# Two-block transformer forward on one core: the gated recurrence computed two chunks to a tile, its steps dealt out between tiles of the weight products

## What is computed

```
b = cumsum(log_f) within a chunk                       # chunks; per head, 128 channels
A[t,s] = sum_d q[t,d] k[s,d] exp(b[t,d] - b[s,d]),  s <= t
o = A v + (q exp(b)) S ;  S' = exp(b_last) S + (k exp(b_last - b))^T v
y_hg = rmsnorm(o) * sigmoid(go) * silu(z)
kc, vc = compress(k), compress(v)                      # 31 overlapping blocks, a two-layer MLP
o_cmp = softmax(q kc^T) vc ;  o_nsa = g0 o_cmp + g1 o_selected + g2 o_window
```

## Time and profile before

| | |
|---|---|
| median of 3 runs | 2809.46 us (2808.98 to 2810.98) |
| the profiled execution | 2808.89 us |
| its span, first to last instruction | 2807.1 us |
| mean granted TensorE clock | 0.991 of full speed |
| PE busy | 2705.7 us (96% of the span) |
| DVE, ACT, POOL busy | 1167.6, 1275.7, 1402.6 us |
| PE's part in the chain that ended last | 85% (DVE 6%, issue 4%, ACT 4%) |

### The profile page before, as it was taken

How to read it: one execution, slowest core, us unless ns; L and a number is a source line. 1 busy time by engine, 2 the same in 40 slices (tenths; PEclk the granted TensorE clock), 3 DMA queues, 4 the chain that set the end, 5 groups by cost and what they waited for, 6 DMA issues and landing times.

```text
span 2807.1 us, 41389 instructions
## 1 busy us (share of the span) xinstructions
PE 2705.7 (96%) x13644; PEld 2276.7 (81%) x13644; DVE 1167.6 (42%) x2054; ACT 1275.7 (45%) x2207; POOL 1402.6 (50%) x1801
## 2 busy tenths in 40 slices
PE   8999899999889999999999999999999999999998
PEld 6888778788877888888878888888888887888887
DVE  4768742567874224423242422322442324142232
ACT  5555745655673643444443432324344444343233
POOL 4535554543554453554634655545355463455553
PEclk9999999999999999999999999999999999999999
DMA  5223013322301332233422333333223342233332
GB/s 153 72 50 99 16 39 90 91 61 65 92 1 54 89 110 69 90 98 98 124 87 69 106 104 91 98 98 110 69 90 98 98 124 88 68 106 105 91 98 98
DMA packets 270818, 242.46 MB, mean 86 GB/s; under 512 B 29376, under 2 KB 203648, under 8 KB 270592
## 3 DMA queue, kind: packets, MB, share of 16 engines
q1 hardware_dynamic: 267696, 235.12, 28.9%
q10 hardware_dynamic: 2896, 4.52, 0.5%
HBM read 237.51 MB, written 2.10 MB: 85 GB/s over the span
## 4 chain that ended last, share of the span: by engine, by line
PE 85%; DVE 6%; issue 4%; ACT 4%; DMA 0%; DVEq 0%; POOL 0%; ACTq 0%; POOLq 0%
PE bank L2017 11%; PE bank L2021 11%; PE bank L2020 11%; PE bank L1951 8%; PE bank L1954 8%; PE bank L1955 8%; PE bank L845 4%; PE bank L849 4%; PE bank L848 4%; PE bank L983 2%; PE bank L1906 2%; PE bank L895 1%; PE bank L898 1%; PE bank L899 1%; PE bank L2142 1%
## 5 line engine op out<-in xcount | busy, mean ns | idle before, releaser
L2865 POOL TENSOR_TENSOR wboth<-raw,wboth 128x256 fp32r<-128x256 f32 (+1 forms) x1616 | 1292.3, 832 | 1289.4 <-ACT wboth L2166 1289.1
L2166 ACT CAST wboth<-raw 128x1024 fp32r<-128x1024 f32 (+2 forms) x443 | 455.4, 1034 | 601.2 <-PE bank L2017 401.9
L1951 PE MATMUL bank<-xhi,wboth 128*128 128x512 f32 x928 | 364.2, 392 | 2.1 <-DVE h L2553 1.6
L1955 PE MATMUL bank<-xhi,wboth 128*128 128x512 f32 x928 | 361.4, 389 | 0.0
L1954 PE MATMUL bank<-xlo,wboth 128*128 128x512 f32 x928 | 361.3, 389 | 0.0
L2017 PE MATMUL bank<-wboth,xhi 128*128 128x512 f32 x832 | 326.5, 392 | 3.9 <-DVE xlo L2444 3.9
L2021 PE MATMUL bank<-wboth,xlo 128*128 128x512 f32 x832 | 324.0, 389 | 0.0
L2020 PE MATMUL bank<-wboth,xhi 128*128 128x512 f32 x832 | 323.8, 389 | 0.0
L845 PE MATMUL bank<-wboth,xhi 128*128 128x512 f32 (+2 forms) x672 | 248.2, 369 | 5.5 <-DVE pT L1524 3.1
L848 PE MATMUL bank<-wboth,xhi 128*128 128x512 f32 (+2 forms) x672 | 243.4, 362 | 0.0
L849 PE MATMUL bank<-wboth,xlo 128*128 128x512 f32 (+2 forms) x672 | 243.4, 362 | 0.0
(11 more groups left out here) (512 smaller groups left out, 4878.2 us busy)
## 6 DMA issues: line engine op xcount, KB each, us to landing
raw<-in_w_in SPq DMA_DIRECT2D x147, 512.0 KB, 3.7
raw<-in_w SPq DMA_DIRECT2D x132, 512.0 KB, 3.8
raw<-in_w_pg SPq DMA_DIRECT2D x16, 512.0 KB, 3.8
raw<-in_w_o SPq DMA_DIRECT2D x16, 512.0 KB, 3.8
raw<-in_xa_k SPq DMA_DIRECT2D x16, 512.0 KB, 3.9
raw<-in_xa_v SPq DMA_DIRECT2D x16, 512.0 KB, 3.9
raw<-in_xa_q SPq DMA_DIRECT2D x16, 512.0 KB, 4.1
raw<-in_xa_o SPq DMA_DIRECT2D x16, 512.0 KB, 3.8
```

The costliest lines, as they stand in the source:

```text
L1951: mm = pe.matmul(o, wh, rhs[0][:, k, :], start=(k == 0), stop=False)
L1955: mm = pe.matmul(o, wl, rhs[0][:, k, :], start=False, stop=(k == KD - 1))
L2166: nc.scalar.copy(whi[:, j % SLOTS, 0:nk * cols], raw[:, j % SLOTS, 0:nk * cols]).then_inc(hi_split, 1)
L2865: ins = nc.gpsimd.tensor_tensor(wlo[:, s, part], raw[:, s, part], whi[:, s, part].bitcast(F32), ALU.subtract)
```

## The change

1. **Pairs.** Chunks 0 and 2 are kept in natural order, chunks 1 and 3 reversed in time, in `qT`, `kT` and `bT` (order 0, 2, 1, 3: `PLACE`). At a level the later half of a natural chunk and the later half of a reversed one occupy different halves of a tile, so one 128x128 product serves both chunks. `level_product` makes two products for a level instead of four; `keep` copies 128x256 instead of 128x512 into a sum tile `Ap` (new masks take both corners); `part_chunks` then splits `Ap` into `At` once per head with two COPY_PREDICATED of 128x256. The diagonal keeps four products and takes two copies. The values of the reversed chunks are reversed once by four products with a reversed identity (`v_back`), emptied by four copies on ACT. Copies of q, the exp that makes kT, and the forward decays take two instructions each instead of one.
2. **Dealing.** tm steps of this stretch are split into parts of one token tile (`part`), and `spread_in` lays them between side steps by `NEEDED`, a table of weights for the side steps, instead of by their number.
3. **Order.** Head 0's decays are made right behind `forget_late` (`hg_decays`); the next head's decays and first level begin inside the present head (`hg_next`, and levels counted through over heads); `hg_out`, its sum and its scaling become three steps that stand 2 to 5 levels into the next head; sums of squares of the queries get steps of their own (`q_sum`). A level's tile is emptied two levels behind, also over the border of two heads. On ACT, last parts, outputs and keys are put a level or two later (`scalar_order`).
4. **Compression.** `c_hid` and `c_back` of the second half stand ahead of `q_rope`, `nz_exp` behind `c_out`; compressed attention has two empty slots, and begins earlier for the next query tile.
5. Small: scratch tiles are shared (`sums`, `coef`, `lbraw`, `lbs`), the mask load has 1280 instead of 1024 columns, one DMA of 128x128 (`back`) is added per layer.

```diff
@@ constants, layout helpers
-        masks[:, lv, :] = (i // (2 * m) == j // (2 * m)) & (i // m % 2 == 0) & (j // m % 2 == 1)
-    masks[:, LEVELS, :] = i == j
+        masks[:, lv, :] = (i // (2 * m) == j // (2 * m)) & (i // m != j // m)
+    masks[:, LEVELS, :], masks[:, LEVELS + 1, :], masks[:, LEVELS + 2, :] = i == j, i < j, i >= j
+PLACE = (0, 2, 1, 3)
+def across(t, m, later):
+    at = lambda o, apart, inner: bass.AP(tensor=t.tensor, offset=t.offset + o, ap=[t.ap[0], [apart, 2], [2 * m, P // m], inner])
+    return at(m, 2 * P - m, [1, m]) if later else at(0, 2 * P + m, [1, m]), at(m - 1, 2 * P + 1, [0, m])
+def paired(t, m, later):
+    return bass.AP(tensor=t.tensor, offset=t.offset + (m if later else 0), ap=[t.ap[0], [-m if later else m, 2], [2 * m, P // m], [1, m]])
@@ the list of steps
+NEEDED = {"hg_prep": 0.4, "hg_level": 2.2, "hg_next": 1.6, "hg_kv": 1.0, "hg_sum": 0.9, "hg_norm": 1.6, "z_gate": 2.1, "hg_out": 0.9, "q_sum": 0.7}
+def spread_in(main, side):
+    tiles = [(("part", step, tt), step[-1][2] * step[-1][4]) for step in main for tt in range(TT)]
+    work, columns = sum(NEEDED.get(step[0], 0) for step in side), sum(n for _, n in tiles)
+    out, sent, asked = [], 0, AHEAD
+    for step in side:
+        asked += NEEDED.get(step[0], 0) * columns / work
+        while tiles and sent + tiles[0][1] / 2 < asked:
+            part, n = tiles.pop(0)
+            out.append(part)
+            sent += n
+        out.append(step)
+    return out + [part for part, _ in tiles]
...
-        return [("c_score", qt), ("c_exp", qt), ("c_weigh", qt), ("c_split", qt), ("c_turn", qt)]
+        return [("c_score", qt), ("c_exp", qt), ("c_weigh", qt), None, ("c_split", qt), None, ("c_turn", qt)]
-            if qt and kt == 0 and (g, br) == (0, 0):
-                compressed = compressed_steps(qt)
+            if qt < TT - 1 and kt == qt // 2 and (g, br) == (1, qt > 0):
+                compressed = compressed_steps(qt + 1)
...
-    s += merged_in(main[2:], side, 2)
+    s += main[2:4] + spread_in(main[4:], side)
-    s += hid[0] + [("k_turn",), ("c_back", 0), ("q_rope",)] + hid[1] + [("nz_exp", 0), ("nz_gate", 0), ("c_back", 1)]
-    s += [("nz_exp", 1), ("c_out",), ("nz_gate", 1)]
+    s += hid[0] + [("k_turn",), ("c_back", 0)] + hid[1] + [("c_back", 1), ("q_rope",), ("c_out",)]
+    s += [("nz_exp", 0), ("nz_gate", 0), ("nz_exp", 1), ("nz_gate", 1)]
@@ PE
+            def step_v_back(step):
+                for tt in range(1, TT, 2):
+                    pe.wait_ge(*G.evacuated(("v", tt), l))
+                    for x in range(2):
+                        name = ("vb", tt, x)
+                        pe.wait_ge(*G.free(name, l))
+                        pe.matmul(G.ps(name)[:, 0:2 * P], back, v[:, tt, 2 * P * x:2 * P * (x + 1)], start=True, stop=True).then_inc(*G.full(name))
-                level_product(("A", hh, lv), Kl[:, lv % 2], Ql[:, lv % 2])
+                level_product(("A", hh, lv), Kl[:, (LEVELS * hh + lv) % 2], Ql[:, (LEVELS * hh + lv) % 2], TT // 2)
@@ DVE
-                tt_(dr, right, mid, ALU.subtract)
-                tt_(dl, mid, left, ALU.subtract).then_inc(*d_ready.up())
+                (later, middle), (earlier, _) = (across(bT[:, hh, :], m, x) for x in (True, False))
+                tt_(paired(dE[:, g % 2, 0:T // 2], m, True), later, middle, ALU.subtract)
+                tt_(paired(dE[:, g % 2, T // 2:T], m, False), middle, earlier, ALU.subtract).then_inc(*d_ready.up())
...
-                nc.vector.copy_predicated(At[:, hh % 2, :, :], masks[:, lv, :].unsqueeze(1).to_broadcast([P, TT, P]),
-                                          G.ps(name)[:, :].rearrange("p (c t) -> p c t", c=TT)).then_inc(*G.empty(name))
+                ps = G.ps(name)[:, :].rearrange("p (z c t) -> p z c t", z=2, c=TT // 2)
+                for z, dst in enumerate((At[:, hh % 2, 0:2, :], Ap[hh % 2]) if lv == LEVELS else (Ap[hh % 2],)):
+                    ins = nc.vector.copy_predicated(dst, masks[:, lv, :].unsqueeze(1).to_broadcast([P, TT // 2, P]), ps[:, z])
+                ins.then_inc(*G.empty(name))
+            def part_chunks(hh):
+                for z in range(2):
+                    ins = nc.vector.copy_predicated(At[:, hh % 2, 2 * z:2 * z + 2, ::-1 if z else 1],
+                                                    masks[:, LEVELS + 1 + z, :].unsqueeze(1).to_broadcast([P, TT // 2, P]), Ap[hh % 2])
+                ins.then_inc(*parted.up())
```

325 lines of the change are left out of this document (204 added, 121 removed).

## The result

The changed kernel takes **2793.88 us** (median of 4 runs, 2792.55 to 2798.04), the kernel before beside it 2809.39; the ratio is 0.9944 (95% interval 0.9932 to 0.9955). It is faster, but by 15.5 us and not by 44: it lies 6 us above the range and 4 us above the rival in which only the products count. The profiled execution is the slowest of the four, 2798.04 us; the others' spans are 4 to 5.5 us shorter.

What follows compares the result with a forecast made beforehand. PE, busy 96% of the span, was taken as the bound, so its work plus gaps set the time. Terms summed to -21.9 us per layer, -43.8 for two, from 2808.9 to 2765 us; range 2748 to 2788.

Steps and rivals of the forecast that it cites:

- Level products, -12.5: Recurrence: 112 of 224 level instructions go at 0.111 us each, -12.5 us per layer, all on PE's path.
- `v_back`, +1.8, and Dealing, +1.3: Recurrence, per layer: four added reversal products cost PE 1.8 us; more returns from side work, 36 against 20, cost 1.3.
- Gaps of the recurrence, -4.4: Recurrence: weight products between levels remove 4.4 of PE's 7.9 us of gaps per layer; bounds 0 and -7.9.
- Clock of the stretch, -1.1: Recurrence: the 0.71 clock in the 5 us from 185 goes with the gap before it, -1.1 us per layer.
- DVE, 97.5 us: Recurrence: DVE's work becomes 97.5 us, its share rising from 71% to 79%: nearer, but not the bound.
- Rival 2: Recurrence: DVE becomes the bound and its pair forms get slower, at 1.1 us each about 2835 us; chance 0.05.
- ACT, nothing: Recurrence: ACT's added copies and split instructions, under 6 us on 74 of 141, stay hidden under weight products.
- Compression ahead of the queries' turn, with the first turn -4.0: Compression and first compressed turn: first exp about 1.6 us sooner, a 2.7 us gap and half clock reduced; -4.0 per layer.
- Rival 3: Before `c_score`: a new gap of some 3 us throws the clock, 2.5 us lost per layer, 2770 us; chance 0.10.
- Compressed probabilities, -3.0 for the three: Attention: free slots end the waits at the other three compressed turns, 6.9 us, of which -3.0 per layer counted.
- Rival 1: Whole kernel: only the products count, gaps shift but stay; -9.4 us per layer, 2790 us; chance 0.22.
- The first rule against the change: Recurrence: DVE and POOL exclude one another; POOL's 56 us in a stretch 11% shorter meet DVE more often.

Runs made afterwards that it cites:

- e8: Base with every level product issued twice into the same places (112 records more per layer): 2800.7 us.
- base: The changed kernel with the compression's old order, the new slots kept (the same run as e1): 2791.1 us.
- e10: Base with the dealing undone: side steps spread by number between whole steps of four tiles, as in the kernel before: 2801.3 us.
- e3: The changed kernel with both the compression's order and the compressed branch's slots put back as in the kernel before: 2794.0 us.
- e1: The changed kernel with the compression's order of before, the new slots kept: 2791.1 us.
- e2: The changed kernel with the compressed branch's slots and starts of before, the compression's new order kept: 2798.1 us.
- e5: The changed kernel with the two z exponentials moved from ahead of the keys' copies, one before the second c_back, one behind the first softmax exponentials: 2791.8 us.
- e18: The changed kernel with c_turn 1, 2 and 3 one slot later, its order and early decays kept: 2788.8 us.
- e12: Base with the levels' kept copies taking 16 of each 128 columns, so most of the recurrence's chunk products are left out: 2790.5 us.
- e13: The kernel before with each level product issued for two of its four tiles, so most of the recurrence's results are missing: 2797.9 us.
- e9: Base with ScalarE's weight casts made two steps of products ahead instead of three, in both blocks: 2856.4 us.

## Why the prediction was wrong

**Level products, -12.5**: right as TensorE's time (10.3 to 10.8 us busy in the stretch; over the whole kernel e8 has 23.0 us more work at full clock than base, 0.103 us for each of 224), wrong as "all of it PE's own time and so on the path". 3.4 to 4.8 us of it became idle time. This is the step that failed in the recurrence: I took the idle time of before as a fixed 7.9 us, and subtracted from it and from the work both. A gap is what a chain on other engines takes beyond the work that PE has meanwhile, and products are part of that work. The profile had a warning for the other way in which products turn into waits: DVE's 8.1 us of idle time before line 1675 was mostly a wait for PE; with less work on PE, it became a wait for ACT, which serves casts at PE's pace.

**`v_back`, +1.8, and Dealing, +1.3**: the busy time in the windows, 123.3, is the forecast 123.5. Dealing alone costs no busy time that e10 shows.

**Gaps of the recurrence, -4.4**: the dealing does take 4.6 us (e10 against base). But it takes them from 12.4, not from 7.9; what I wrote as a result, 3.5 us of gaps, was never there to have. The term was right, the missing one is +3.4 to +4.8. **Clock of the stretch, -1.1**: in the first layer there is no gain, the dip moved from 185 us to 205; in the second it went, with 2.9 us. Together that is near the forecast, by luck: in e3 and e1 the second layer's dip is gone too, in e2, e5 and e18 it is there.

**DVE, 97.5 us**: 99.8. (That the second layer is alike to a tenth holds for PE, not for DVE: 99.7 and 98.4 us before.) Copies of 256 cost 0.44, against 0.46; the pair forms cost about as much as plain ones; `part_chunks` took 0.72 a copy, seven of the eight beside POOL. Rival 2 is dead, and e12 shows that the time of the copies hardly counts. What DVE does in one place counts: 5.7 us of it without a pause stand ahead of the longest gap. **ACT, nothing**: as an amount of work it is right (73.0 us busy). As an order it was the fault: its exponentials stand behind casts, its keys' copies behind z's exponentials.

**Compression ahead of the queries' turn, with the first turn -4.0**: measured +1.4 to +2.1 per layer for the order (e1 to e3). This is the second step that failed, and with the slots it is half of what is missing. "I reckon the first exp about 1.6 us sooner" failed: 0.1. I had counted ACT's wait of 1.16 us as gain and overlooked that the two z exponentials (3.8 us), which before stood between the compression's own steps while these were on PE and DVE, now stand behind all of them and right ahead of the keys' copy. Rival 3 is what happened here: a gap of 3.45 us before `c_score`, then a clock of 0.50 to 0.55. I had priced it at 2.5 us; in this execution it is (1 - 0.55) x 3.75 + (1 - 0.50) x 5.0 = 4.2.

**Compressed probabilities, -3.0 for the three**: the slots bring 1.5 to 2.1 per layer. "It will be late with the next thing too" was right, and the next thing is named: the bank of a turned tile.

**The rivals.** Rival 1, with 0.22, came nearest (2790). The profile is as it had it, work down and idle time unmoved; that idle time stands still as the sum of two opposite moves, and that the clock takes 9 us, it did not have. The first rule against the change counted for more than I gave it, which was nothing in the sum. The Trainium skill, SBUF — State Buffer, section "Who interferes with whom", has a VectorE instruction with two SBUF inputs and a GpSimd instruction that reads SBUF exclude one another. The trace agrees: 0.94 us for one form while POOL's pieces run, 0.42 without them. In the mean over the stretch it changed little (0.54 to 0.61 us against 0.49 to 0.57), but four such instructions in a row stand ahead of the stretch's longest gap.

**What no term had**: 9 us more lost to the clock, tails that are longer behind an earlier start even with the code of before (3.1 us in e3), and block two 4.9 us longer. Part of it may belong to the one profiled execution; the cause was not found.

**The signs that I had named**: "gaps stay at 8 us" and "the first exp comes no sooner" were the two that fired.

## What to carry to other kernels

Work taken from the engine that is 96% busy is not worth its time if it was what covered the chains of the others, or if its feeders run at its pace. Ask for each gap which work of the busy engine lies over the late engine's chain, and whether the late engine had waited for the busy one a little earlier; what goes from that cover comes back as idle time (here a third, e8, to nearly a half, e13, of what was saved). In an in-order engine look at what stands ahead of the awaited instruction and what *that* waits for; its busy share did not tell here (ACT 56% in the stretch). When a step moves to an earlier slot, find out who had its PSUM bank last and how long ago.

## What was not expected of the hardware

Block two's code is the same, yet its length differed between the profiled executions: from the last `c_val` to the end 1925.2 us before, 1930.1 in the changed kernel, 1933.1 in e1, 1925.7 in e8. There is one profiled execution of each kernel, and runs of one kernel lie 2 to 9 us apart, so whether the length goes with the kernel or with the execution is not shown. It is as large as most differences argued above. One piece is at the start of its second pass: PE stands for "issue", that is for nothing that the profile shows, for 1.5 us, and the granted clock is 0.71 in the 5 us from 1875. Before, the like pause was 0.5 us. The shift between the two kernels went there from -14.8 to -11.6 us.

```profile
1874.26 0.44 PE L2114 MATMUL bank<-xhi,wboth 128*128 128x512 f32 x1 [1.47 <-issue]
```

What makes that pause was not tried. Nor was a ring of five weight slots, which might take the casts' wait away without the late low parts of e9.
